# Feed-forward blocks of a one-core encoder layer: running sums copied by ScalarE from PSUM bank to PSUM bank, another order of the seven products, two of four weight sums on VectorE

## The reference, cut to what matters

```
u = rmsnorm(h, pre_norm)                       # 512 x 1024
y = (silu(u @ w_gate) * (u @ w_up)) @ w_down   # w_gate, w_up: 1024 x 2816, w_down: 2816 x 1024
h = h + 0.5 * rmsnorm(y, post_norm)
```

## Time and profile before

| | |
|---|---|
| median of 3 runs | 1253.93 us (1246.37, 1255.10, 1253.93) |
| the profiled execution | 1248.43 us, span 1246.6 us |
| mean granted TensorE clock | 0.986 of full speed |
| PE busy | 1190.0 us, 95% of the span |
| DVE, ACT, POOL busy | 854.9 us, 572.5 us, 397.4 us (69%, 46%, 32%) |
| stage of the change, block 1 and block 2 | 56.7 to 267.2 us and 841.0 to 1051.2 us of the span |

### The profile page before, as it was taken

The page is one execution under the profiler, slowest core; times in us unless marked ns, Lnnn a source line. Parts: engine busy times, 40 slices in busy tenths (PEclk is TensorE's granted clock), DMA queues, the critical chain, the costliest instruction groups (busy, mean ns, idle before and its releaser), DMA issues.

```text
span 1246.6 us, 17852 instructions
## 1 busy us (share of the span) xinstructions
PE 1190.0 (95%) x6860; PEld 1023.1 (82%) x6860; DVE 854.9 (69%) x1165; ACT 572.5 (46%) x885; POOL 397.4 (32%) x255
## 2 busy tenths in 40 slices
PE   9999899899999999999999999999998998999998
PEld 8889898888888886657887888788988988888887
DVE  6988878873334797765567873798888787333584
ACT  6544444443234636566343632654443444232473
POOL 6457657600002300000112102447657562000245
PEclk9999999989998999999999999999999999999998
DMA  6322323232332232111522233323323224223211
GB/s 212 102 74 95 101 70 99 101 102 102 101 92 54 66 108 64 45 41 35 153 85 69 85 102 101 101 70 100 101 70 98 84 85 135 91 95 101 101 35 68
DMA packets 101855, 112.00 MB, mean 90 GB/s; under 512 B 15294, under 2 KB 91678, under 8 KB 101542
## 3 DMA queue, kind: packets, MB, share of 16 engines
q1 hardware_dynamic: 97542, 109.18, 28.2%
q10 hardware_dynamic: 4256, 2.12, 0.6%
HBM read 108.12 MB, written 3.16 MB: 89 GB/s over the span
## 4 chain that ended last, share of the span: by engine, by line
PE 69%; DVE 14%; issue 8%; ACT 7%; DMA 1%; SPq 0%; POOL 0%; DVEq 0%; ACTq 0%
PE bank L303 14%; PE bank L305 13%; PE bank L304 13%; PE bank L780 4%; PE bank L782 4%; PE bank L781 4%; DVE w_lo L920 3%; DVE scratch L868 3%; DVE prod L878 3%; ACT w_hi L908 3%; PE bank L626 2%; PE bank L620 2%; PE bank L621 2%; ACT scratch L883 1%; PE bank L310 1%
## 5 line engine op out<-in xcount | busy, mean ns | idle before, releaser
L337 DVE TENSOR_TENSOR w_lo<-w_raw,w_hi 128x1024 fp32r<-128x1024 f32 x121 | 156.2, 1297 | 180.8 <-ACT w_hi L330 180.4
L330 ACT ACTIVATE w_hi<-w_raw 128x1024 fp32r<-128x1024 f32 x121 | 126.2, 1054 | 197.4 <-PE bank L305 191.5
L780 PE MATMUL bank<-T_hi,w_hi 128*128 128x256 f32 x576 | 170.2, 295 | 42.2 <-ACT scratch L1043 42.2
L781 PE MATMUL bank<-T_lo,w_hi 128*128 128x256 f32 x576 | 166.0, 288 | 0.0
L782 PE MATMUL bank<-T_hi,w_lo 128*128 128x256 f32 x576 | 165.9, 288 | 0.0
L780 PEld LDWEIGHTS bank<-T_hi,w_hi 128*128 128x128 f32 x576 | 113.6, 197 | 48.8 <-ACT scratch L1043 48.7
L303 PE MATMUL bank<-T_hi,w_hi 128*128 128x512 f32 x352 | 138.0, 392 | 4.2 <-DVE w_lo L337 4.2
L304 PE MATMUL bank<-T_lo,w_hi 128*128 128x512 f32 x352 | 137.6, 391 | 0.0
L305 PE MATMUL bank<-T_hi,w_lo 128*128 128x512 f32 x352 | 137.5, 391 | 0.0
L303 PE MATMUL bank<-v_hi,w_hi 128*128 128x512 f32 x328 | 132.8, 405 | 0.0
L305 PE MATMUL bank<-v_hi,w_lo 128*128 128x512 f32 x328 | 128.2, 391 | 0.0
(11 more groups left out here) (312 smaller groups left out, 2703.8 us busy)
## 6 DMA issues: line engine op xcount, KB each, us to landing
w_raw<-in_ffn_w_up SPq DMA_DIRECT2D x44, 512.0 KB, 3.9
w_raw<-in_ffn_w_down SPq DMA_DIRECT2D x44, 512.0 KB, 3.5
w_raw<-in_ffn_w_gate SPq DMA_DIRECT2D x43, 512.0 KB, 4.2
w_raw<-in_w_in SPq DMA_DIRECT2D x32, 512.0 KB, 3.6
w_raw<-in_w_out SPq DMA_DIRECT2D x8, 512.0 KB, 3.4
w_raw<-in_ple_w_gate SPq DMA_DIRECT2D x8, 512.0 KB, 3.3
x_tm<-in_x SPq DMA_DIRECT2D x4, 512.0 KB, 8.1
Mb<-m_rows ACTq DMA_DIRECT2D x8, 256.0 KB, 5.1
```

The costliest lines, as they stand in the source:

```text
L330: nc.scalar.activation(w_hi[:, s, :], w_raw[:, s, :], ACT.Copy).then_inc(w_hi_done, 1)
L337: nc.vector.tensor_tensor(w_lo[:, s, :], w_raw[:, s, :], w_hi[:, s, :].bitcast(F32), ALU.subtract).then_inc(w_lo_done, 1)
L780: nc.tensor.matmul(o, whi, a_hi(kk), start=(start and kk == 0), stop=False, skip_group_check=True)
L781: nc.tensor.matmul(o, whi, a_lo(kk), start=False, stop=False, skip_group_check=True)
```

## The change

- **Products.** All products use the left half (256 columns) of a bank. The order is: 1 (g0, A11) to b; 2 (g2, S1 with T1) to b+2; 3 (g2, S2 with T2) onto b; 4 (g1, A12) onto b+1; 5 (g3, S3 with T3) onto b; 6 (g3, S4) onto b+3; 7 (g1, A22 with T4) onto b+2.
- **Copies.** ACT's copies go from PSUM to PSUM: copy 1, after product 1, b to b+1; copy 3, after product 3, b to b+3; copy 4, after product 5, b to b+2. Copy 2, after product 2, takes b+2 to a quarter of `scratch` (`r5`). Products 3, 5 and 7 wait for copies 1, 3 and 4. PE adds the products that DVE added before.
- **Weight sums.** POOL makes S1 and S3, DVE makes S2 and S4 (`sum_dve`). Groups: g2 = S1, S2; g3 = S3, S4 (before: S1, S3 and S2, S4). The groups are written in the order g0, g2, g3, g1, and g1 of the next quad only after product 7.
- **DVE's posts.** `left_dve` (twice) scales or multiplies the left token half straight from PSUM, `right_dve` (twice) adds `r5` to a bank for the right half, `close_dve` scales or multiplies the right half (2 x 256 columns, SBUF only). `gate_scale_dve` and `prod_dve` remain for the two lead blocks.
- **Loads.** The raw loads of a quad wait for the low part of all four groups of the quad two before, g1 being the last.
- The wait of the first copy for `prod` is gone. `s_dve` is a new semaphore; the counts of the others follow.

The diff, without the hunk of the semaphore counts and that of the two lead-only functions, and cut where bodies that are printed above are removed:

```diff
@@ -702,7 +702,8 @@
         T1, T2, T4, T3 = range(4)
-        FREED = (1, 5, 6, 7)
+        FREED = (1, 7, 3, 6)
+        ORDER = (0, 2, 3, 1)
         POST0 = 8
@@ -754,15 +755,17 @@
                         qd = 2 * (i - LEADS - 1) + j // 2
-                        own.wait(sp, "s_sum", 4 * qd + 4)
-                        own.wait(sp, "s_lo", 4 * qd + 2)
+                        own.wait(sp, "s_sum", 2 * qd + 2)
+                        own.wait(sp, "s_dve", 2 * qd + 2)
+                        own.wait(sp, "s_lo", 4 * qd + 4)
                     sp_load(sp, i, j)
...
                     qd = QUADS - 2 + k // 2
-                    own.wait(sp, "s_sum", 4 * qd + 4)
-                    own.wait(sp, "s_lo", 4 * qd + 2)
+                    own.wait(sp, "s_sum", 2 * qd + 2)
+                    own.wait(sp, "s_dve", 2 * qd + 2)
+                    own.wait(sp, "s_lo", 4 * qd + 4)
                 else:
@@ -771,19 +774,22 @@
-            def product(g, off, step, a_hi, a_lo, bank, half, start):
+            def product(g, off, step, a_hi, a_lo, bank, start):
                 s = (N + g) % RING
...
                     whi, wlo = w_hi[:, s, c:c + P], w_lo[:, s, c:c + P]
-                    o = B[b + bank][:, 256 * half:256 * half + 256]
+                    o = B[b + bank][:, 0:256]
                     nc.tensor.matmul(o, whi, a_hi(kk), start=(start and kk == 0), stop=False, skip_group_check=True)
...
             def weights(g):
-                own.wait(pe, "s_lo", 8 * i + (4 * q + g + 1 - 8 * LEADS))
+                own.wait(pe, "s_lo", 8 * i + (4 * q + ORDER.index(g) + 1 - 8 * LEADS))
+            def copied(c):
+                own.wait(pe, "rcopy", 8 * i + (4 * q + c - 8 * LEADS))
@@ -794,22 +800,23 @@
             weights(0)
-            product(0, 0, P, *v(0, 0), 0, 0, True)
-            weights(1)
-            product(1, 0, 2 * P, *v(1, 0), 1, 0, True)
+            product(0, 0, P, *v(0, 0), 0, True)
             weights(2)
             own.wait(pe, "t_lo", T1 + 1)
-            product(2, 0, P, *T(T1), 2, 1, True)
+            product(2, 0, P, *T(T1), 2, True)
+            own.wait(pe, "t_lo", T2 + 1)
+            copied(1)
+            product(2, 4 * P, P, *T(T2), 0, False)
+            weights(1)
+            product(1, 0, 2 * P, *v(1, 0), 1, False)
             weights(3)
-            own.wait(pe, "t_lo", T2 + 1)
-            own.wait(pe, "rcopy", 6 * i + (3 * q + 1 - 6 * LEADS))
-            product(3, 0, P, *T(T2), 0, 0, False)
+            own.wait(pe, "t_lo", T3 + 1)
+            copied(3)
+            product(3, 0, P, *T(T3), 0, False)
+            product(3, 4 * P, P, *v(1, 1), 3, False)
             own.wait(pe, "t_lo", T4 + 1)
-            product(1, P, 2 * P, *T(T4), 2, 0, False)
-            own.wait(pe, "t_lo", T3 + 1)
-            own.wait(pe, "rcopy", 6 * i + (3 * q + 2 - 6 * LEADS))
-            product(2, 4 * P, P, *T(T3), 0, 0, False)
-            product(3, 4 * P, P, *v(1, 1), 3, 0, True)
+            copied(4)
+            product(1, P, 2 * P, *T(T4), 2, False)
@@ -890,15 +891,19 @@
+        S1, S2, S3, S4 = (wsum[:, a, :, :] for a in range(4))
         def group_hi(act, qd, g):
...
             if qd == QUADS:
-                hi_upto(act, DN + g)
+                if g == 0:
+                    hi_upto(act, DN)
                 return
...
             else:
-                own.wait(act, "s_sum", 4 * qd + 2 * g - 2)
+                own.wait(act, "s_sum", 2 * qd + g - 1)
+                own.wait(act, "s_dve", 2 * qd + g - 1)
             if qd == 0:
@@ -910,9 +915,10 @@
             if qd == QUADS:
-                lo_upto(dve, DN + g)
+                if g == 0:
+                    lo_upto(dve, DN)
                 return
-            own.wait(dve, "s_hi", 4 * qd + g + 1)
+            own.wait(dve, "s_hi", 4 * qd + ORDER.index(g) + 1)
             src, c = group_ap(g, qd % 2)
@@ -945,7 +951,7 @@
             if k < 4:
-                own.wait(act, "mm", 7 * (QUADS - 1) + 3 + k // 2)
+                own.wait(act, "mm", 7 * (QUADS - 1) + 2 + k // 2)
             else:
@@ -955,28 +961,51 @@
-        def posts_dve(dve, qd, stage):
+        def sum_dve(dve, qd, e):
+            if qd == QUADS:
+                return
+            A11, A12, A21, A22 = raw_blocks(qd % 2)
+            own.wait(dve, "s_sum", 2 * qd + 1)
+            if e == 0:
+                nc.vector.tensor_tensor(S2, S1, A11, ALU.subtract).then_inc(own["s_dve"], 1)
+            else:
+                own.wait(dve, "s_dve", 2 * qd + 1)
+                nc.vector.tensor_tensor(S4, A12, S2, ALU.subtract).then_inc(own["s_dve"], 1)
+        t0, t1 = slice(0, 256), slice(256, 512)
+        def r5(q):
+            return scratch[:, 2 + q, t0]
+        def left_dve(dve, qd, m):
+            q, p = qd % 2, LEADS + qd // 2
+            psum = B[4 - 4 * q + (1, 2)[m]][:, t0]
+            own.wait(dve, "mm", 7 * qd + (4, 7)[m])
+            if q == 0:
+                nc.vector.tensor_tensor(scratch[:, m, t0], psum, r_b[:, t0], ALU.mult).then_inc(own["post"], 1)
+            else:
+                own.wait(dve, "silu_done", p + 1)
+                nc.vector.tensor_tensor(prod[:, 2 * p + m, t0], psum, scratch[:, m, t0], ALU.mult).then_inc(own["post"], 1)
+        def right_dve(dve, qd, m):
             q = qd % 2
...
+            psum = B[4 - 4 * q + (3, 0)[m]][:, t0]
+            own.wait(dve, "mm", 7 * qd + (6, 5)[m])
+            own.wait(dve, "rcopy", 4 * qd + 4)
+            nc.vector.tensor_tensor(scratch[:, 2 * q + m, t1], psum, r5(q), ALU.add).then_inc(own["post"], 1)
+        def close_dve(dve, qd):
+            q, p = qd % 2, LEADS + qd // 2
+            own.wait(dve, "post", POST0 + 4 * qd + 4)
+            X = scratch[:, 2 * q:2 * q + 2, t1]
+            if q == 0:
+                nc.vector.tensor_tensor(X, X, r_b[:, None, t1].broadcast_to([P, 2, 256]), ALU.mult).then_inc(own["gate_scaled"], 1)
             else:
...
+                nc.vector.tensor_tensor(prod[:, 2 * p:2 * p + 2, t1], X, scratch[:, 0:2, t1], ALU.mult).then_inc(own["prod_ready"], 1)
@@ -992,29 +1021,31 @@
                 T_lo_dve(dve, x)
+            sum_dve(dve, 0, 0)
             group_lo(dve, 0, 0)
-            group_lo(dve, 0, 1)
+            sum_dve(dve, 0, 1)
             gate_scale_dve(dve, 1)
...
             group_lo(dve, 0, 3)
+            group_lo(dve, 0, 1)
             prod_dve(dve, 1)
...
             for qd in range(QUADS):
-                posts_dve(dve, qd, 0)
                 group_lo(dve, qd + 1, 0)
-                posts_dve(dve, qd, 1)
-                group_lo(dve, qd + 1, 1)
-                posts_dve(dve, qd, 2)
+                sum_dve(dve, qd + 1, 0)
+                sum_dve(dve, qd + 1, 1)
                 group_lo(dve, qd + 1, 2)
+                left_dve(dve, qd, 0)
+                right_dve(dve, qd, 1)
+                right_dve(dve, qd, 0)
                 if qd == QUADS - 1:
                     plo_dve(dve, 0)
-                posts_dve(dve, qd, 3)
                 group_lo(dve, qd + 1, 3)
-                if qd % 2 == 0:
-                    gate_scale_dve(dve, LEADS + qd // 2)
-                else:
-                    prod_dve(dve, LEADS + qd // 2)
+                left_dve(dve, qd, 1)
+                close_dve(dve, qd)
+                group_lo(dve, qd + 1, 1)
+            lo_upto(dve, DN + 3)
             for k in range(1, 4):
@@ -1032,18 +1063,13 @@
-        def r_copy_act(act, qd, e):
...
+        def copy_act(act, qd, e):
+            b = 4 - 4 * (qd % 2)
+            own.wait(act, "mm", 7 * qd + (1, 2, 3, 5)[e])
+            src = B[b + 2 if e == 1 else b][:, t0]
+            dst = (B[b + 1][:, t0], r5(qd % 2), B[b + 3][:, t0], B[b + 2][:, t0])[e]
+            nc.scalar.activation(dst, src, ACT.Copy).then_inc(own["rcopy"], 1)
@@ -1059,24 +1085,26 @@
             group_hi(act, 0, 0)
-            group_hi(act, 0, 1)
             lead_out_act(act, 1, 0)
...
             group_hi(act, 0, 3)
+            group_hi(act, 0, 1)
             lead_out_act(act, 1, 1)
             for qd in range(QUADS):
-                r_copy_act(act, qd, 0)
+                copy_act(act, qd, 0)
                 group_hi(act, qd + 1, 0)
...
                     silu_act(act, LEADS + qd // 2)
-                r_copy_act(act, qd, 1)
-                group_hi(act, qd + 1, 1)
-                r_copy_act(act, qd, 2)
+                copy_act(act, qd, 1)
+                copy_act(act, qd, 2)
                 group_hi(act, qd + 1, 2)
...
                     phi_act(act, 0)
+                copy_act(act, qd, 3)
                 group_hi(act, qd + 1, 3)
+                group_hi(act, qd + 1, 1)
+            hi_upto(act, DN + 3)
             for k in range(1, 4):
@@ -1094,19 +1122,15 @@
                 A11, A12, A21, A22 = raw_blocks(qd % 2)
-                S1, S3, S2, S4 = (wsum[:, a, :, :] for a in range(4))
                 for e in range(2):
...
                 if qd >= 1:
+                    own.wait(pool, "s_lo", 4 * (qd - 1) + 2)
```

(62 more changed lines are left out.)

## The result

The changed kernel took 1209.14 us (median of 4 runs, 1207.48 to 1210.8), the kernel before beside it 1250.15 us (median of 4, 1244.2 to 1255.1). The ratio is 0.967, with a 95% interval from 0.962 to 0.973: 3.3% faster. The profiled execution took 1209.79 us, with a span of 1207.9 us and a mean granted clock of 0.995; before it was a span of 1246.6 and 0.986.

What follows compares the result with a forecast made beforehand. PE, busy 95% of the span, was taken to set the end, losing time in the two quad stages. 1248.4 - 57.9 + 11 + 3 = 1204.5 us, plus 2 for the median, gave 1206 us, range 1189 to 1230.

Steps and rivals of the forecast that it cites:

- the loop: Quad stages: g1 written last ties loads, POOL's sums, DVE and PE into a 10.3 to 10.4 us turn; +11 us.
- the lead: Start of each block's quads: hi g1 ahead of copy 1 makes product 3 1.7 us late; +3 us in all.
- the end of a stage: Three high parts move behind product 7, but PE has 5.8 us of ready matmuls first; nothing lost.
- The 2 us added for the median: Added to the sum of 1204.5 us, which lay 5.5 us under the median of the three runs before.
- The waits that go: Both quad stages: PE's waits for ACT's copies, their restarts and the slower clock go; 57.9 us of excess.
- The copies in PSUM: ACT's copies 1, 3 and 4: 0.38 us each as into SBUF, hidden with 0.8 us of cover.
- The rival of a dear copy: PE waits at products 3, 5 and 7 if PSUM copies exceed 1.19 us; 1292 us at 2.0 us each; chance 0.05.
- my upper bound (+30): The loop if loads land after 5.75 us, S1 behind lo g3: 0.9 us x 34 = +30.
- No new loop: Rival: loads land early enough, or S1 comes before hi g3 is done; 1196 us, chance 0.2.
- The clock falls all the same: Rival: one short idle per quad lowers PE's clock, 1.7 us in one of three quads; 1226 us, chance 0.06.
- Late loads at full price: Rival: loads land late, so POOL's S1 stands behind lo g3; 1225 us, chance 0.16.
- Silu: Rival: the wait moves to silu, making copies 2 to 4 late in up quads; 1215 us, chance 0.08.

Runs made afterwards that it cites:

- Experiment 1: Kernel before, with a second SBUF tile for the gate half of every second pair, so the first copy waits for an earlier `prod`: 1204.43 us, ratio 0.962.
- experiments 7: Kernel before, with the second gate tile and silu behind ACT's second copy instead of ahead of it: 1201.55 us, ratio 0.960.
- 10: Kernel before with second gate tile and later silu, all four POOL sums cut to 16 columns from the second quad on: 1188.53 us, one run.
- Experiment 4: Changed kernel, with POOL's S3 waiting for the low part of g1 instead of g3 of the quad before: 1185.77 us, ratio 0.947.
- Experiments 2: Changed kernel, with POOL's S1 and S3 cut to 16 of 512 columns from the second quad on: 1185.7 us, one run.
- 6: Changed kernel, with half of the rows of each block of raw loads left out from the third block on: 1186.14 us, one run.
- experiment 9: Kernel before with second gate tile and later silu, plus `prod`'s first high and low parts made ahead of g1's in the last quad: 1194.62 us, ratio 0.955.
- experiment 8: Changed kernel, with the low part of g1 ahead of the close on DVE: 1194.11 us, one run.

## Why the prediction came out right

1206 was said and 1209.1 measured, within the range. The mechanism and its place were right. Three sizes were off: the loop cost 13 us more than forecast, the lead 1.4 less and the end of a stage 6 less. Together that is 5.6 us, which takes the sum of 1204.5 to 1210.1, beside 1209.8 in the profiled execution. The 2 us added for the median had no counterpart afterwards: the profiled execution lies within 0.7 us of the median now. That the forecast came within 3 us is therefore partly luck. Of the signs named, stages of 188 to 190 us and waits of 0.2 to 0.3 us at product 4 were not met; they were 194.4 and 193.9 us, and 0.53 us on average.

- *The waits that go* (57.9 us of excess, the lower clock included): right, and no stretch of the lower clock is left in the stages. Experiment 1 shows the wait for the tile alone, with 41.8 us of it. The prediction named only that wait and silu behind it; that POOL's sums would have kept the old order at 10.45 us a quad all the same (experiments 7 and 10) it did not say.
- *The copies in PSUM* (0.38 us, hidden): right, 0.368 against 0.377 into SBUF. The page "ScalarE: Activation LUTs" of the Trainium skill (Step-by-step: what each stage is for) says that PSUM is the faster; the trace agrees by 9 ns only, so the rule decided nothing. The rival of a dear copy is refuted.
- *The loop* (+11 us): right in every member, as it was in the place of PE's wait and in what holds DVE; mis-sized, about +24. Its legs from S1 to S3 and from S3 to the next issue were forecast at 2.46 and 3.06 us (4.85 to 7.31, 7.31 to 10.37) and measured 2.46 and 3.07. The number that was off is the load: 4.78 us from issue to S1 were said, 5.31 measured. I had read the end of the traffic, where the start of the waiting engine was wanted. Half a microsecond is small beside 10, but the lateness is a difference: it went from 0.3 us a quad to 0.8 (10.87 - 10.08), in 30 of 36 quads. Experiment 4 takes out 23 us with one number, which confirms the size. It was between my middle and my upper bound (+30).
- *No new loop* (1196): didn't come by itself. Experiments 2, 4 and 6 reached it and came to 1186, 10 us below. The next two terms give 7.4 of these, the 2 us added for the median the rest.
- *The lead* (+3 us): the right wait (60.20, for copy 1), half the size: 0.8 us late a block. Silu had been done sooner, so hi g3 ran at 56.80 instead of 57.83 and hi g1 filled ACT's former idle time.
- *The end of a stage* (nothing): this step failed. I followed the high parts that move behind product 7, but not what moves ahead: `prod`'s first low part had stood behind two weight splits and made PE wait 2.1 us in each block. That gave -6 us; experiment 9, which makes only that split earlier, gave 6.9 by the medians and 5.5 by the spans. I had not looked at the waits just behind the stages.
- *The sum of these*: -57.9 + 24 + 1.6 - 6 = -38.3, the span's -38.7. Outside them stretches of lower clock stand at different places in the two profiles, even where PE was busy for at least 0.99 of every us just before (393 to 400 us before, 1133 to 1141 after, some 3.4 us lost in either); they cancel here.
- *The clock falls all the same*: refuted. 30 idles of 0.3 to 0.7 us, one in nearly every quad, and a granted clock of 1.00 there. The trace doesn't bear out for this kernel what the page "TensorE: Matmul & The Clock Gate" of the Trainium skill (A second HAM failure mode: psum-queue depth-cycling) says of short idles between groups of matmuls.
- *Late loads at full price*: not come; lo g3 lasts 1.73 to 2.14 us in every turn behind the first quads, so S1 began ahead of it each time. *Silu*: not come, but in experiment 8.

## What to carry to other kernels

Before a new order or a new place for data, try the one tile more that ends the reuse wait: here it was worth as much as the whole change. When two engines hold each other up, write down the loop with the start of each instruction; its period follows from the starts, not from the busy shares, and one wait that picks another victim for the hold can be worth 23 us. Take landing times from when a waiting engine went on, not from the end of the traffic, and read the waits just outside the stage that changes.
